# Router logits with the weights held stationary, attention loads issued inside the expert rounds, and key-value products interleaved with their transposes

## The chip, the cores and the metric

One core of one Trainium2 chip. The metric is the device time of one execution in microseconds (us), as the median of several runs. All data are float32; where a product must be exact the kernel splits operands itself.

## What is computed

A two-layer encoder over 16 learned meta tokens followed by 512 frames, width 1024 (48 pad positions in front are inert). Layer 0 is multi-scale retention plus a mixture of experts; after it one shared key/value is projected from the residual stream; layer 1 is sliding-window attention over that shared key/value plus a second mixture of experts; a last RMSNorm follows. The parts that the change touches:

```python
def hier_moe(h, w_group, w_router, w_gate, w_up, w_down):      # twice
    t = h.reshape(-1, d)
    g_probs = jax.nn.softmax(t @ w_group, axis=-1)             # 4 groups
    e_logits = (t @ w_router).reshape(-1, 4, 4)                # 16 experts
    ...                                                        # top group, top 2 experts in it
def shared_kv(x, kv_norm, kv_w, kv_b, pos):                    # once, between the layers
    kv = rms_norm(x, kv_norm) @ kv_w + kv_b                    # 1024 x 512
    ...
q = rope((rms_norm(h, swa_norm) @ w_q + b_q), pos)             # 1024 x 1024
```

## The kernel before

**Tiles and stages.** Tokens lie in five tiles: tile 4, called META, with the 16 meta tokens, and tiles 0 to 3 with 128 frames each. The program runs in this order, each engine with its own hand-written list: retention (four heads, in `head` on every engine); `experts(0)`; the norm before attention, keys and values, queries; attention over four tiles; `experts(1)`; the last norm. Every matrix product needs its input feature-major, so after each norm TensorE transposes a tile in eight blocks into two PSUM banks (`transposed`, L725 to L734), and VectorE multiplies them by the norm's gains into `xT` (`gained`, L1300 and `feature_major`, L1306).

**Banks.** PSUM has 8 banks of 128 x 512. The class `Fills` counts how often each bank was filled and read; `fl.phase` gives names to banks in the order of use, and `wait_full`, `wait_free`, `wait_read` wait on the counts. `norm_plan` (L367) deals the tiles of a norm over four bank pairs.

**The router** (`experts(l)` on TensorE, L868 to L879). All tiles are transposed (L732), then for every tile eight products give its logits, 20 columns (4 groups and 16 experts). The token features `xT` are the stationary operand there and the router weights `wr` the moving one, so that the result is token-major, as VectorE's selection of experts wants it (L1457 on). The selection ends in a rank for every token, an indirect DMA that scatters the rows, and a one-hot product (L890) that builds the rows of round 0 directly. Both kernels have that one-hot product.

**Expert rounds.** 16 rounds of about equal length. In each, two experts with up to 64 rows each are worked on: gate and up product (L913), hidden (L1645), down product (L932). The SyncE queue (SP) loads weights into five slots (`gu`, L449: three lie in `ring`, two in the arena), ahead of the rounds; ScalarE's queue loads rows (L1199) and stores results (L1216). `PASSES` (L42) says which experts a round takes: round k has the second block of expert k-1 and the first of k+1.

**Between the layers.** POOL gathers the experts' results (L1869); per tile VectorE adds them to `h` (L1670, L1672), ScalarE squares (L1069), POOL makes the deviation (L1826, L1829), VectorE scales (L1297), TensorE transposes (L732), VectorE multiplies the transposed tile with the key-value gains into `xTk` and then with the query gains into `xT` (`kv_features`, L1681). When all five tiles are there, TensorE makes keys and values (L959) and then the first tile's queries (L968). SP loads `w_kv` into `ring[:, 0]`, five tables, and the two halves of `w_q` into `ring[:, 1]` and `ring[:, 2]` after the last gathered tile has been used (L697 to L705).

Of the kernel before, what the change touches and what calls it, by code (L numbers as in the profile page):

```python
# [24 lines left out]
META = NT  # L25
# [24 lines left out]
def pass_of(kind, j):  # L50

    return next(p for p, halves in enumerate(PASSES) if (kind, j) in halves)

# [141 lines left out]
def build(nc, a, out):  # L195
# [4 lines left out]
    with ctx:  # L200
# [106 lines left out]
        yo = cv(2, D)  # L307
        th, hid1, hid = cv(2, FF), cv(FF), cv(2, FF)
# [58 lines left out]
        def norm_plan(tag, tiles):  # L367
            fl.phase([(f"{tag}{t}", 2 * (n % 4)) for n, t in enumerate(tiles)])
# [28 lines left out]
        norm_plan("n1_", TILES5)  # L397
        t_norm1 = list(fl.total)
        fl.phase([(f"KV{t}", n) for n, t in enumerate(TILES5)])
        fl.phase([("Qa0", 6), ("Qb0", 7)])  # L400
        fl.phase([(f"KT{t}", (5, 0, 1, 2, 3)[n]) for n, t in enumerate(TILES5)])
# [27 lines left out]
        def sigs(names, tag):  # L429
# [10 lines left out]
            "swa_tables_in", "k_rotated", "V_ready", "VX_zeroed", "VX_ready"))  # L440
        q_rot, m_ready, p_exp, snk_exp, p_scaled, first_parts_used, k_padded, bo_added = (sem(n) for n in (
# [156 lines left out]
        def _(sp):  # L598
# [55 lines left out]
            def experts(l):  # L654
# [43 lines left out]
            sp.dma_start(ring[:, 0], a["w_kv"][0]).then_inc(kv_in, 16)  # L698
            for dst, src in ((stab, a["t_swa"]), (sink_b, a["swa_sinks"][0].partition_broadcast(128)),
                             (kvb, a["kv_b"].partition_broadcast(128)),  # L700
                             (qb, a["swa_b_q"][0].partition_broadcast(128)),
                             (bo, a["swa_b_o"][0].partition_broadcast(128))):
                sp.dma_start(dst, src).then_inc(s_swat, 16)
            for c in range(2):
                sp.dma_start(ring[:, 1 + c], a["w_q"][c]).then_inc(q_in[c], 16)  # L705
# [16 lines left out]
        def _(pe):  # L722
# [145 lines left out]
            def experts(l):  # L868
# [3 lines left out]
                for n, t in enumerate(tiles):  # L872
                    fl.wait_read(pe, f"m{l}_{t}")
                    if n == 0:
                        fl.wait_free(pe, f"LG{l}")
# [1073 lines left out]
```

## Time and profile before

| | |
|---|---|
| median of 3 runs | 1374.65 us (1372.19 to 1377.16) |
| the profiled execution, its own time | 1370.72 us |
| its span, first to last instruction | 1368.7 us |
| mean granted TensorE clock | 0.917 of full |
| TensorE busy (matmul) | 1166.4 us, 85% |
| VectorE, ScalarE, GpSimd busy | 474.0, 244.9, 239.1 us |
| chain that ended last, by engine | PE 66%, issue 12%, DVE 12%, POOL 5%, DMA 3% |
| that chain, lines of this change | L959 3%, L877 2%, L968 4% (with all query products) |

The span counts from the first to the last instruction; what lies around it is 2 us. The chain of waits is followed back from the last instruction, so its shares say what the time consists of; busy shares only say what an engine did meanwhile. "issue" is time in which the engine waited for nothing that the profile shows. In the trace each float32 product of the program is two MATMUL instructions, so that 40 products stand as x80.

### The profile page before, as it was taken

Reading aid. Unit: us, or ns where it says so; the run is one execution under the profiler, and the core shown is the slowest. Engines: PE = TensorE matmul, PEld = TensorE weight load, DVE = VectorE, ACT = ScalarE, POOL = GpSimd, SP = SyncE. Lnnn points to the kernel's source line nnn. Section 1 sums busy time; section 2 is a strip of 40 time slices with the busy share of each in tenths; the row PEclk is TensorE's granted clock in tenths of the full one; section 3 lists DMA queues with packets and bytes.
Section 4 is the critical chain, followed back from the end, with each engine's and each line's share of the span. In section 5 each row is a group of like instructions: output and inputs, shape, how many; then the busy total and the mean of one; then the engine's idle time right before and its main releaser. Section 6 shows DMA issues by size and latency. Waiting matters only on the chain.

```text
span 1368.7 us, 15208 instructions
## 1 busy us (share of the span) xinstructions
PE 1166.4 (85%) x5784; PEld 725.9 (53%) x5784; DVE 474.0 (35%) x847; ACT 244.9 (18%) x453; POOL 239.1 (17%) x168
## 2 busy tenths in 40 slices
PE   4899999999998998489999927877887748999990
PEld 4889889789696776433333313343443343333330
DVE  5301432332258203512222246264554462222224
ACT  4122132132142112000111110021321400101111
POOL 4233233143044221020000044000000002000004
PEclk8999999999999999589999957979999869999995
DMA  6131141041140124649999346300011084999935
GB/s 250 62 139 62 47 154 62 31 169 62 46 154 1 62 82 201 256 142 306 354 346 339 89 154 238 123 0 1 1 67 56 1 338 157 320 355 359 321 86 215
DMA packets 38673, 212.30 MB, mean 155 GB/s; under 512 B 5376, under 2 KB 5504, under 8 KB 29648
## 3 DMA queue, kind: packets, MB, share of 16 engines
q1 hardware_dynamic: 21168, 151.26, 29.8%
q10 hardware_dynamic: 12704, 43.13, 10.2%
q0 software_dynamic: 4736, 17.04, 3.4%
q8 instruction: 41, 0.67, 0.2%
q14 instruction: 24, 0.20, 0.0%
HBM read 307.75 MB, written 35.78 MB: 251 GB/s over the span
## 4 chain that ended last, share of the span: by engine, by line
PE 66%; issue 12%; DVE 12%; POOL 5%; DMA 3%; ACT 2%; ACTq 0%; POOLq 0%; DVEq 0%
PE ps L744 20%; PE ps L913 16%; PE ps L932 8%; PE ps L968 4%; PE ps L1054 4%; POOL ring_r L1838 4%; PE ps L959 3%; PE ps L901 2%; PE ps L877 2%; PE ps L830 2%; DVE xT L1303 1%; DVE arena L1765 1%; DVE arena L1768 1%; PE ps L890 1%; DMA xT<-slot_rows 1%
## 5 line engine op out<-in xcount | busy, mean ns | idle before, releaser
L913 PE MATMUL ps<-ring,xT 128*64 128x512 f32 x640 | 226.9, 598 | 5.9 <-DVE xT L1303 5.9
L744 PE MATMUL ps<-x_hi,ring_r 128*128 128x264 f32 x1024 | 191.3, 287 | 7.0 <-DVE xT_r L1291 7.0
L1838 POOL TENSOR_TENSOR ring_r<-ring,ring_r 128x1024 fp32r<-128x1024 f32 x56 | 134.1, 2408 | 301.9 <-ACT ring_r L1081 301.9
L913 PE MATMUL ps<-arena,xT 128*64 128x512 f32 x384 | 168.7, 592 | 0.0
L744 PE MATMUL ps<-ring_r,x_hi 128*128 128x512 f32 (+1 forms) x480 | 156.2, 407 | 11.6 <-POOL ring_r L1838 11.6
L744 PEld LDWEIGHTS ps<-x_hi,ring_r 128*128 128x128 f32 x1024 | 160.6, 190 | 7.5 <-DVE xT_r L1291 7.3
L1303 DVE TENSOR_TENSOR xT<-ps,gains 128x512 f32<-128x512 f32 (+1 forms) x100 | 62.0, 665 | 249.6 <-PE ps L901 247.3
L744 PE MATMUL ps<-xT_r,ring_r 128*128 128x264 f32 x512 | 146.3, 286 | 0.0
L932 PE MATMUL ps<-arena 128*64 128x512 f32 x512 | 118.6, 606 | 6.1 <-ACT arena L1204 6.1
L913 PEld LDWEIGHTS ps<-ring,xT 128*64 128x64 f32 x640 | 72.9, 138 | 95.4 <-issue 92.0
L744 PEld LDWEIGHTS ps<-ring_r,x_hi 128*128 128x128 f32 (+1 forms) x480 | 84.6, 177 | 43.2 <-POOL ring_r L1838 13.1
L744 PEld LDWEIGHTS ps<-xT_r,ring_r 128*128 128x128 f32 x512 | 97.1, 190 | 0.1
L1869 POOL DMA_INDIRECT arena<-slot_out,slot_i x18 | 17.6, 977 | 413.1 <-DMA slot_out<-arena 408.3
L913 PEld LDWEIGHTS ps<-arena,xT 128*64 128x64 f32 x384 | 52.6, 137 | 54.8 <-issue 54.8
L1081 ACT ACTIVATE ring_r<-ring 128x1024 fp32r<-128x1024 f32 x56 | 57.7, 1052 | 123.7 <-PE ps L744 73.7
L932 PEld LDWEIGHTS ps<-arena 128*64 128x64 f32 x512 | 35.2, 138 | 66.9 <-issue 66.9
L968 PE MATMUL ps<-ring,xT 128*128 128x512 f32 x128 | 60.9, 638 | 9.2 <-DVE arena L1765 9.2
L744 PE MATMUL ps<-ring_r,xT_r 128*128 128x512 f32 (+1 forms) x160 | 65.0, 406 | 0.0
L732 PE MATMUL ps<-con,arena 128*128 128x128 f32 (+1 forms) x152 | 24.5, 324 | 42.0 <-DVE arena L1297 40.2
L1204 ACT ACTIVATE arena<-ps 128x256 f32<-128x256 f32 x32 | 12.3, 384 | 259.2 <-PE ps L920 252.8
L1826 POOL TENSOR_SCALAR var<-ss 128x1 f32<-128x1 f32 (+1 forms) x23 | 9.1, 397 | 262.4 <-ACT arena L1069 254.7
L968 PEld LDWEIGHTS ps<-ring,xT 128*128 128x128 f32 x128 | 25.8, 204 | 42.8 <-issue 42.8
(225 smaller groups left out, 1481.9 us busy)
## 6 DMA issues: line engine op xcount, KB each, us to landing
ring<-in_w_gu SPq DMA_DIRECT2D x46, 2048.0 KB
arena<-in_w_down SPq DMA_DIRECT2D x74, 1024.0 KB
arena<-in_w_gu SPq DMA_DIRECT2D x28, 2048.0 KB
ring<-in_w_ret SPq DMA_DIRECT2D x48, 512.0 KB, 3.6
slot_out<-arena ACTq DMA_DIRECT2D x64, 256.0 KB, 7.1
xT<-slot_rows ACTq DMA_DIRECT2D x60, 256.0 KB, 5.1
slot_rows<-arena ACTq DMA_DIRECT2D x8, 1024.0 KB, 4.1
ring<-in_w_ret_out SPq DMA_DIRECT2D x16, 512.0 KB, 4.5
```

Of the source, the lines that this page charges most:

```text
L744: last = mm(dst, a_parts[x], b_parts[y], start=(start and n == 0), stop=(stop and n == 2))
L830: last = mm(ps[:, b + g, c - lo:HALF], v_tm[0:r, t, 128 * m:128 * m + 128], scores_of(t)[0:r, c - 128 * t:hi - 128 * t], start=(t == 0), s ...
L877: last = mm(ps[0:rows(t), 0, 20 * t:20 * t + 20], xT[:, k, col0(t):col0(t) + rows(t)], wr[:, l, k, :], start=(k == 0), stop=(k == KT - 1))
L901: last = nc.tensor.transpose(ps[:, c // 4, 128 * (c % 4):128 * (c % 4) + 128], xg[:, k % 2, 128 * c:128 * c + 128], ident)
L913: last = mm(ps[cols, b, :], xgT[:, k % 2, c, cols], by_row(gu(j))[:, c, :], start=(c == 0), stop=(c == KT - 1))
L932: last = mm(ps[cols, b, :], hidT[:, c, cols], down[:, j % W_SLOTS, c, 512 * n:512 * n + 512], start=(c == 0), stop=(c == 1))
L959: last = mm(ps[0:rows(t), b, :], xTk[:, k, col0(t):col0(t) + rows(t)], w_kv[:, k, :], start=(k == 0), stop=(k == KT - 1))
L968: last = mm(ps[:, b, :], xT[:, k, col0(t):col0(t) + 128], w_q[c][:, k, :], start=(k == 0), stop=(k == KT - 1))
L1054: last = mm(ps[:, 4 + c, :], oT1[:, k, :], w[:, k, :], start=(k == 0), stop=(k == KT - 1))
L1081: nc.scalar.activation(w_hi[to][:, m], w_raw[slot][:, m], ACT.Copy).then_inc(hi_made, 1)
L1303: return V_.tensor_tensor(dst[:, 4 * g:4 * g + 4, c0:c0 + r], src, gains[:, gain, 4 * g:4 * g + 4].unsqueeze(2).to_broadcast([128, 4, r]), ...
L1838: G.tensor_tensor(w_lo[slot][:, m], w_raw[slot][:, m], w_hi[to][:, m], ALU.subtract).then_inc(lo_made, 1)
```

## The change

It has three parts.

**Router, both layers.** The weights `wr` (20 columns) become the stationary operand and the features the moving one, 128 columns; the logits come out feature-major, 20 x 128, in banks 4 and 5 by turns. ScalarE copies each to `logit_f`, and TensorE transposes them back, one small product per tile, into bank 6. The transposes use two bank pairs instead of four, and the logits of a tile are issued behind the transposes of the next one.

**Loads.** SP issues the five tables in round 8 of layer 0, behind a wait for the scatter; `w_q`'s second half in round 12, `w_kv` in round 13, and `w_q`'s first half in round 15 (`last_use(1)`, `last_use(2)`, `last_use(0)`).

**Keys and values.** The product of a tile is issued behind the transposes of the next one, as in the router. The query features move from VectorE to ScalarE, eight activations of 128 x 128 per tile, with the gain as scale.

```diff
+def last_use(slot):
+    return max(pass_of("second", j) for j in range(slot, EXPERTS, W_SLOTS))
...
+        logit_f = arena[:, cv.at:cv.at + POS]
...
-            norm_plan(f"m{l}_", MOE_TILES[l])
-            fl.phase([(f"LG{l}", 0), (f"RK{l}", 2), (f"X0_{l}", 0)])
+            fl.phase([(f"m{l}_{t}", 2 * (n % 2)) for n, t in enumerate(MOE_TILES[l])])
+            fl.phase([(f"LT{l}_{t}", 4 + n % 2) for n, t in enumerate(MOE_TILES[l])])
+            fl.phase([(f"LG{l}", 6), (f"RK{l}", 2), (f"X0_{l}", 0)])
...
-        norm_plan("n1_", TILES5)
+        norm_plan("n1_", TILES5, 2)
...
@@ SP @@
                 for k in range(ROUNDS):
                     round_full(sp, l, gu_bank(k), k)
                     next_weights(gate_up_weights, k)
+                    beside(k)
...
-            experts(0)
-            sp.wait_ge(mo[0]["gath_used"], 5)
-            (the same loads)
+            def attention_loads(k):
+                if k == EXPERTS // 2:
+                    sp.wait_ge(mo[0]["scattered"], 16 * 2 * 5)
+                    for dst, src in ((stab, a["t_swa"]), (sink_b, ...), (kvb, ...), (qb, ...), (bo, ...)):
+                        sp.dma_start(dst, src).then_inc(s_swat, 16)
+                if k == last_use(2):
+                    sp.dma_start(ring[:, 0], a["w_kv"][0]).then_inc(kv_in, 16)
+                for c in range(2):
+                    if k == last_use(c):
+                        sp.dma_start(ring[:, 1 + c], a["w_q"][c]).then_inc(q_in[c], 16)
+            experts(0, attention_loads)
...
@@ TensorE, experts(l) @@
-                transposed(f"m{l}_", tiles, xn, nrm[f"_m{l}"])
-                for n, t in enumerate(tiles):
-                    fl.wait_read(pe, f"m{l}_{t}")
-                    for k in range(KT):
-                        last = mm(ps[0:rows(t), 0, 20 * t:20 * t + 20], xT[:, k, col0(t):col0(t) + rows(t)],
-                                  wr[:, l, k, :], start=(k == 0), stop=(k == KT - 1))
-                last.then_inc(full[0], 1)
+                def logits(t):
+                    c, b, r = col0(t), fl.bank(f"LT{l}_{t}"), rows(t)
+                    fl.wait_read(pe, f"m{l}_{t}")
+                    fl.wait_free(pe, f"LT{l}_{t}")
+                    for k in range(KT):
+                        last = mm(ps[0:20, b, 0:r], wr[:, l, k, :], xT[:, k, c:c + r], start=(k == 0), stop=(k == KT - 1))
+                    last.then_inc(full[b], 1)
+                def logits_to_tokens(t):
+                    fl.wait_read(pe, f"LT{l}_{t}")
+                    return nc.tensor.transpose(ps[0:rows(t), 6, 20 * t:20 * t + 20], logit_f[0:20, col0(t):col0(t) + rows(t)],
+                                               ident[0:20, 0:20])
+                for n in range(len(tiles) + 1):
+                    if n < len(tiles):
+                        transposed(f"m{l}_", tiles, xn, nrm[f"_m{l}"], tiles[n])
+                    if n:
+                        logits(tiles[n - 1])
+                for t in tiles:
+                    last = logits_to_tokens(t)
+                last.then_inc(full[6], 1)
...
@@ TensorE, keys and values @@
-            transposed("n1_", TILES5, xn1, nrm["_s"])
-            pe.wait_ge(kv_in, 16)
-            all_read(pe, t_norm1)
-            for t in TILES5: (the eight products of a tile)
+            for n in range(len(TILES5) + 1):
+                if n < len(TILES5):
+                    transposed("n1_", TILES5, xn1, nrm["_s"], TILES5[n])
+                if n:
+                    key_values(n - 1, TILES5[n - 1])    # waits kv_in and kv_x_ready >= n
...
@@ ScalarE @@
+            def query_features(n, t):
+                b, c = fl.bank(f"n1_{t}"), slice(col0(t), col0(t) + rows(t))
+                act.wait_ge(kv_x_ready, n + 1)
+                for k in range(KT):
+                    last = nc.scalar.activation(xT[:, k, c], ps[:, b + k // 4, 128 * (k % 4):128 * (k % 4) + 128], ACT.Copy,
+                                                scale=gains[:, G_SWA, k:k + 1])
+                last.then_inc(free[b], 1)
...
@@ VectorE, kv_features @@
-                if t != META:
-                    for gx in range(2):
-                        last = gained(xT, b, gx, G_SWA, col0(t), rows(t))
-                last.then_inc(free[b], 1)
+                last.then_inc(kv_x_ready, 1)
```

How the instructions move on TensorE in the router of layer 0. `con,arena` is a transpose (identity and normed rows), `wr,xT` the old logits; the line numbers of the changed kernel are its own. Before:

```order
1536 L732 MATMUL ps<-con,arena 128x128 x32
1537 L732 MATMUL ps<-con,arena 128x16 x8
1538 L877 MATMUL ps<-wr,xT 128x20 x32
1539 L877 MATMUL ps<-wr,xT 16x20 x8
1540 L883 MATMUL ps<-arena,con 128x80
```

and now:

```order
1536 L748 MATMUL ps<-con,arena 128x128 x16
1537 L892 MATMUL ps<-xT,wr 20x128 x8
1538 L748 MATMUL ps<-con,arena 128x128 x8
1539 L892 MATMUL ps<-xT,wr 20x128 x8
1540 L748 MATMUL ps<-con,arena 128x128 x8
1541 L892 MATMUL ps<-xT,wr 20x128 x8
1542 L748 MATMUL ps<-con,arena 128x16 x8
1543 L892 MATMUL ps<-xT,wr 20x128 x8
1544 L892 MATMUL ps<-xT,wr 20x16 x8
1545 L898 MATMUL ps<-con,arena 128x20 x4
1546 L898 MATMUL ps<-con,arena 16x20
```

The logits' products now start behind two tiles' transposes, and five small transposes (L898) stand at the end.

TensorE between the layers, keys and values (`ring,arena`) and the first queries (`ring,xT`). Before:

```order
1787 L732 MATMUL ps<-con,arena 128x16 x8
1788 L732 MATMUL ps<-con,arena 128x128 x32
1789 L959 MATMUL ps<-ring,arena 16x512 x8
1790 L959 MATMUL ps<-ring,arena 128x512 x32
1791 L968 MATMUL ps<-ring,xT 128x512 x16
```

and now:

```order
1794 L748 MATMUL ps<-con,arena 128x16 x8
1795 L748 MATMUL ps<-con,arena 128x128 x8
1796 L988 MATMUL ps<-ring,arena 16x512 x8
1797 L748 MATMUL ps<-con,arena 128x128 x8
1798 L988 MATMUL ps<-ring,arena 128x512 x8
1799 L748 MATMUL ps<-con,arena 128x128 x8
1800 L988 MATMUL ps<-ring,arena 128x512 x8
1801 L748 MATMUL ps<-con,arena 128x128 x8
1802 L988 MATMUL ps<-ring,arena 128x512 x16
1803 L1005 MATMUL ps<-ring,xT 128x512 x16
```

META's product now stands behind tile 0's transposes, where three tiles' transposes stood before it.

The SP queue in round 8 of layer 0, behind that round's gate and up weights (L643), as it is now (`TENSOR_LOAD e_of` reads an expert's number); before, these five table loads stood behind the last round, at L703:

```order
296 L643 DMA ring<-in_w_gu 128x4096
297 L711 DMA arena<-in_t_swa 128x992 [waits scattered_0]
298 L711 DMA arena<-in_swa_sinks 128x16
299 L711 DMA arena<-in_kv_b 128x512
300 L711 DMA arena<-in_swa_b_q 128x1024
301 L711 DMA arena<-in_swa_b_o 128x1024
302 L664 TENSOR_LOAD e_of [waits bank_full7]
```

They stand now ahead of the next down weights, whose expert number is read from the last row on.

## Rows read from the trace of the kernel before

**Rows 1.** Busy time in two stretches; columns are named in the first row
```profile
core 0: us, PE busy (x) PEld busy (x) DVE busy (x) ACT busy (x) POOL busy (x), PEclk, DMA share, GB/s
545.40:560.00 14.60, 14.46 (x80) 14.32 (x80) 0.04 (x1) 0.00 (x0) 0.00 (x0) 0.50 1.02 429
...
793.00:832.50 39.50, 8.76 (x40) 7.20 (x40) 26.17 (x34) 5.75 (x10) 16.57 (x20) 0.52 0.56 193
```

**Rows 2.** Timeline of PE, router of layer 0: start, duration, instruction, [idle before]
```profile
537.68 3.65 PE L732 MATMUL ps<-con,arena 128*128 128x128 f32 x32
541.61 0.64 PE L732 MATMUL ps<-con,arena 16*128 16x16 f32 x8 [0.27 <-DVE arena L1297]
545.46 14.46 PE L877 MATMUL ps<-wr,xT 128*128 128x20 f32 x80 [3.21 <-DVE xT L1303]
```

**Rows 3.** Timeline of DVE, same place
```profile
538.75 1.29 DVE L1303 TENSOR_TENSOR xT<-ps,gains 128x512 f32<-128x512 f32 x2 [0.17 <-PE ps L732]
```

**Rows 4.** Timeline of PE, router of layer 1
```profile
1097.61 2.81 PE L732 MATMUL ps<-con,arena 128*128 128x128 f32 x24 [1.71 <-issue]
...
1101.71 10.49 PE L877 MATMUL ps<-wr,xT 128*128 128x20 f32 x64
```

**Rows 5.** Prices: the chain of waits (head 0), and one line's instructions (ScalarE)
```profile
280.31 1.78 PE ps L798 x8
...
L1204 ACT ACTIVATE arena<-ps x32: 384/384/386, 615.3 to 1331.7; 128x256 f32<-128x256 f32 x32
```

**Rows 6.** Busy time by microsecond, routers of layers 0 and 1; columns of rows 1
```profile
544.00:545.00 1.00, 0.00 (x0) 0.00 (x0) 1.00 (x3) 0.00 (x0) 0.00 (x0) 1.00 0.91 385
...
546.00:547.00 1.00, 1.00 (x7) 1.00 (x6) 0.00 (x0) 0.00 (x0) 0.00 (x0) 0.50 0.97 410
...
1104.00:1105.00 1.00, 1.00 (x12) 1.00 (x11) 0.25 (x1) 0.00 (x0) 0.00 (x0) 1.00 0.97 401
...
1106.00:1107.00 1.00, 1.00 (x7) 1.00 (x6) 0.00 (x0) 0.00 (x0) 0.00 (x0) 0.50 1.04 442
```

**Rows 7.** Timeline between the layers, all engines
```profile
815.19 1.94 PE L732 MATMUL ps<-con,arena 128*128 128x128 f32 x8 [2.17 <-DVE arena L1297]
...
818.94 1.28 DVE L1303 TENSOR_TENSOR arena<-ps,gains 128x512 f32<-128x512 f32 x2
...
823.95 0.34 SPq L698 DMA_DIRECT2D ring<-in_w_kv  x1
...
826.90 0.74 DVE L1297 TENSOR_SCALAR arena<-h,rstd 128x1024 f32<-128x1024 f32 x1
...
832.58 36.15 PE L959 MATMUL ps<-ring,arena 128*16 128x512 f32 x80 [2.84 <-DVE xT L1303]
```

**Rows 8.** The chain of waits behind them: the first queries
```profile
868.73 13.73 PE ps L968 x32
```

**Rows 9.** DMA issues between the layers: count, KB each, us to landing
```profile
ring<-in_w_q SPq DMA_DIRECT2D x2, 2048.0 KB, 17.6
...
ring<-in_w_kv SPq DMA_DIRECT2D x1, 2048.0 KB, 8.2
```

**Rows 10.** Busy time by round, layer 0, around `gate_up` 11 and 14; columns of rows 1
```profile
724.70:736.39 11.69, 10.88 (x56) 4.05 (x54) 2.65 (x5) 0.77 (x3) 0.00 (x0) 1.00 1.02 359
...
759.77:771.46 11.69, 11.69 (x60) 4.43 (x58) 2.73 (x6) 1.25 (x4) 0.00 (x0) 1.00 0.22 56
```

**Rows 11.** The row loads of layer 0's rounds, and the waits of PE there
```profile
DMA to landing us min/median/max: 3.5/5.7/12.1
...
PE ps L901 <- DMA xT<-slot_rows: 0.8, 1, 0.8
```

**Rows 12.** Timeline at 841 us: POOL's bias additions beside VectorE
```profile
841.17 0.68 DVE L1725 TENSOR_TENSOR arena<-ps,arena 16x512 f32<-16x512 f32 x1 [8.74 <-PE ps L959]
...
842.54 4.88 POOL L1878 TENSOR_TENSOR h<-h,arena 128x1024 f32<-128x1024 f32 x2
842.78 4.78 DVE L1710 TENSOR_TENSOR arena<-arena 16x128 f32<-16x128 f32 x2
```

More of the change, by code:

```diff
@@ L365, in build, with norm_plan @@
         A, B, C, E = 0, 2, 4, 6
-        def norm_plan(tag, tiles):
-            fl.phase([(f"{tag}{t}", 2 * (n % 4)) for n, t in enumerate(tiles)])
+        def norm_plan(tag, tiles, pairs=4):
+            fl.phase([(f"{tag}{t}", 2 * (n % pairs)) for n, t in enumerate(tiles)])
         norm_plan("n0_", TILES5)
@@ L396, in build @@
         moe_plan(0)
-        norm_plan("n1_", TILES5)
[L398 to L401, printed above, removed]
+        norm_plan("n1_", TILES5, 2)
+        fl.phase([(f"KV{t}", 4 + n % 4) for n, t in enumerate(TILES5)])
+        fl.phase([("Qa0", 0), ("Qb0", 1)])
+        fl.phase([(f"KT{t}", (2, 3, 5, 6, 7)[n]) for n, t in enumerate(TILES5)])
         t_kv = list(fl.total)
@@ L652, in first_weights, with experts @@
                         down_weights(l, j, j)
-            def experts(l):
+            def experts(l, beside=lambda k: None):
                 def number(row, j, most):
@@ L694, in _ @@
             first_weights(0, (lambda: out_chunk_used(sp, 2), lambda: None, lambda: out_chunk_used(sp, 3)))
-            experts(0)
-            sp.wait_ge(mo[0]["gath_used"], 5)
[L698 to L705, printed above, removed]
+            def attention_loads(k):
+                if k == EXPERTS // 2:
+                    sp.wait_ge(mo[0]["scattered"], 16 * 2 * 5)
+                    for dst, src in ((stab, a["t_swa"]), (sink_b, a["swa_sinks"][0].partition_broadcast(128)),
+                                     (kvb, a["kv_b"].partition_broadcast(128)),
+                                     (qb, a["swa_b_q"][0].partition_broadcast(128)),
+                                     (bo, a["swa_b_o"][0].partition_broadcast(128))):
+                        sp.dma_start(dst, src).then_inc(s_swat, 16)
[5 more added lines that the diff above has]
+            experts(0, attention_loads)
             fl.wait_full(sp, f"KV{TILES5[-1]}")
@@ L723, in _, with transposed @@
             mm = nc.tensor.matmul
-            def transposed(tag, tiles, src, sig):
+            def transposed(tag, tiles, src, sig, only=None):
                 for n, t in enumerate(tiles):
+                    if only is not None and t != only:
+                        continue
                     r, b = rows(t), fl.bank(f"{tag}{t}")
@@ L1062, in _, with squares @@
         def _(act):
-            def squares(tiles, sig, junk, ready):
+            def squares(tiles, sig, junk, ready, only=None):
                 for n, t in enumerate(tiles):
+                    if only is not None and t != only:
+                        continue
                     ready(t)
@@ L1179, in experts @@
                 squares(MOE_TILES[l], nrm[f"_m{l}"], moe_junk[l], ready)
+                for t in MOE_TILES[l]:
+                    b = fl.bank(f"LT{l}_{t}")
+                    fl.wait_full(act, f"LT{l}_{t}")
+                    nc.scalar.activation(logit_f[0:20, col0(t):col0(t) + rows(t)], ps[0:20, b, 0:rows(t)], ACT.Copy)\
+                        .then_inc(free[b], 1)
                 act.wait_ge(m["eg_in"], 1)
```

23 lines of the change are left out of this document (17 added, 6 removed).

## The prediction

> **What bounds the kernel now.** I read the clock and span first (0.917 granted), then the chain of waits, then the timeline of TensorE at the three places where the diff touches it, then busy time in short stretches there, and last the DMA views. The chain is TensorE for two thirds; in the expert rounds TensorE has no gap, so only stages between them can give something. Three of those are touched. In the router of layer 0, 80 logit instructions take 14.46 us [rows 2], all at half the clock and with TensorE nominally busy [rows 1, 6]: each moves 20 columns and loads 128, so it is paid by the load, 0.18 us apiece. In layer 1 the same 64 take 10.49 us [rows 4], 0.164 apiece; the clock falls halfway through them [rows 6]. Between the layers TensorE does 8.76 us of work in 39.5 [rows 1] and then 36.15 us of key-value products in one piece [rows 7]. Those start at 832.58, right behind VectorE's last features, and `w_kv`, issued at 823.95, needs 8.2 us to land [rows 7, 9]: 832.15. Two waits of nearly equal length end there, so removing only one would give almost nothing; the change removes both.
>
> **Prices.** A 128-block transpose costs 3.65/32 = 0.114 us at full clock [rows 2] and 1.94/8 = 0.243 at half [rows 7]. The new logits move 128 columns over 20 loaded ones. The trace of before has no such form. The nearest row is a float32 product that moves 264 columns, 8 instructions in 1.78 us [rows 5], 0.84 ns a column, so 128 columns are 0.108 us at full clock and twice that, 0.216, at half. I take 0.108, since the row is of the same type, bound by moving as this one will be. From above the bound is 0.164 [rows 4], if the load still counted in full; from below 0.054, half the row. The Trainium skill ("TensorE: Matmul & The Clock Gate", Back-to-back issue gap) gives N/2.4 + 2.5 ns, which is 56 ns for 128 columns; its examples are bf16 and this trace does not agree for float32 (264 columns by it are 113 ns, the row has 222). By its figure the eight full tiles' logits of both layers would be worth 16 x 8 x 0.052 = 6.7 us more.
>
> **Router, layer 0.** A tile is 16 instructions: 16 x 0.108 = 1.73 us. TensorE comes free at 537.68 as before [rows 2]; two tiles' transposes, then it waits for tile 0's features, which VectorE ends at 540.04 [rows 3]. From there: four tiles of logits 6.9; transposes of tiles 2 and 3, 16 x 0.114 = 1.8; META's transposes 0.64 [rows 2]; META's logits, 16 instructions of 16 columns, between 0.2 by columns and 1.8 by the price of a transpose, I take 1.0; ScalarE's copy of the last logits at most 0.38 [rows 5], and five small transposes at 0.114, 0.57. Sum 11.3, so the selection starts at 551.3 where the products ended at 559.92. **-8.6 us.** VectorE's features (1.29 a tile [rows 3]) hide under the 2.6 us that TensorE has per tile; if that cover went, the stage would be 1.3 us a tile, still shorter. ScalarE's other copies hide likewise.
>
> **Router, layer 1.** Tile 0's transposes run 1097.61 to 1098.5; its features are ready at about 1099.8. Then four tiles of logits 6.9, two tiles of transposes 1.8, copy and four small transposes 0.84: 1109.4. Before, 1101.71 + 10.49 = 1112.2 [rows 4]. **-2.8 us**: here the old logits ran half warm and began early.
>
> **Keys and values.** META's product needs META's features, tile 0's transposes on TensorE (end 815.19 + 1.94 = 817.13 [rows 7]) and `w_kv`, now issued in round 13. So the block starts at 817.1 instead of 832.58. It takes the same 36.15 us, which already has a cold beginning (80 x 0.429 = 34.3 by the price of the query products, 13.73/32 [rows 8]; the surplus is four instructions at half clock). Into it go the transposes of tiles 1 to 3, 24 x 0.114 = 2.7 us. End 856.0 instead of 868.73. **-12.7 us.** VectorE must keep ahead: tile 0's key features end by 820.2 and are wanted near 826; tile 3's scaled rows came at 827.64 [rows 7] although VectorE then also made the query features (two pairs of 1.28 before it), and are wanted near 841. ScalarE's eight activations per tile cost at most 8 x 0.38 = 3.1 us [rows 5] against 7.8 us per tile on TensorE, and the first query product waits only for the last tile's, near 847, well before 856. So that move is worth nothing by itself and costs nothing. POOL's bias additions, which waited for the tables, now start near 826 beside VectorE's features. Before, two small VectorE instructions with both inputs in SBUF took 4.78 us beside them, while one that read PSUM kept its 0.68 [rows 12]; the features read PSUM, and even 4.8 us would fit into the slack, so I take nothing. What follows (rotation, transposes of keys) keeps its order and moves as a whole. The moves of `w_q` are worth nothing either: issued at 827 it landed 17.6 us later [rows 9], by 845.
>
> **Loads.** 1.8 MB of tables go into round 8, 2 MB each into rounds 12, 13 and 15. Around `gate_up` 11 the DMA share is 1.02 at 359 GB/s; around 14 it is 0.22 [rows 10]. So the tables and the first weights meet full engines: 1.8 MB at 359 GB/s delay what stands behind them on SP by 5.2 us. The expert weights are issued three rounds, some 35 us, ahead and should bear that. Row loads on ScalarE's queue land in 5.7 us, at worst 12.1, and one of them already made TensorE wait 0.8 us [rows 11]; two or three more rounds are now full. I take +0.6 us, between 0 and 11 (all 4 MB in full rounds coming out as waiting). The new wait for the scatter stands in round 8 and was met in round 1; behind it on SP are only weights with three rounds to spare.
>
> **Sum.** -8.6 - 2.8 - 12.7 + 0.6 = -23.5 us. The profiled execution took 1370.72 us; that gives 1347.2. It lies 3.9 below the median of the runs shown, so the median should be 1351.
>
> **Rivals.** (a) *The clock falls in the routers.* The small products may not hold the clock through the waits. With all logits and later transposes at half clock, layer 0 takes 22.5 us from 540 (13.8 + 3.9 + 1.3 + 2 + 1.5), 2.6 more than before, and layer 1 19.2 from 1099.8, 6.8 more: total -12.7 + 9.4 + 0.6 = -2.7, time 1372. For it: the clock fell in layer 1 some 4 us into the old logits, with TensorE busy all along, and in layer 0 behind 3.2 us of waiting [rows 2, 6]. Against: those instructions moved 20 columns each, the new ones move 128, back to back, and the longest wait left is 0.5 us. A fall halfway gives -13, 1361. (b) *The row loads starve.* For it: full engines and the 12.1 us landing. At its bound of +11 instead of +0.6 the time is 1361. The Trainium skill ("DMA: Bandwidth & Descriptors", Issuing engines are not separate DMA queues) speaks for this one: SP's early loads run on the same engines as ScalarE's row loads and interleave with them, so moving them up takes from the rounds; the share of 1.02 agrees. Against: the delay is once, and the rounds from 14 on are empty. (c) *Slower: cold pieces between the layers.* Cut into pieces with transposes between, the key-value work might never get the full clock. At 0.857 us each, 80 instructions are 68.6 us; with 24 transposes at 0.243 they end at 891.5, 22.8 us later than before; with (a), the whole is +32.8, time 1407. By itself it decides where 23.5/0.43 = 55 of the 80 instructions run at half clock (four did). Against: once started, 7 us stretches of 512-column products follow each other with less than 1 us between. (d) *Nothing changes between the layers*, because `w_kv` or the features come late after all: -10.8, 1364.
>
> **Chances.** Forecast 0.75, partial fall of (a) 0.10, full (a) 0.04, (b) 0.05, (c) 0.03, (d) 0.03. A measurement of this kernel tells some 0.3%, 4.1 us, from no change. Faster is all but full (a) and (c), 0.93; same is full (a), 0.04; slower (c), 0.03. The range goes down to 1344 (logits below my price, less cold at the start of the keys, spread of runs) and up to 1362, where the partial fall and (b) lie.
>
> **What would show it.** Logit instructions near 0.108 us apart with the clock at 1.00 through both routers; selection near 551 and, from the new start of its stage, 2.8 us earlier in layer 1; key-value products from 817 to 856 with the first queries right behind; DMA share above 0.9 until about 760, and no wait of TensorE for weights in the rounds. The forecast is wrong if the clock row of a router reads 0.50 from the first logits on, if TensorE waits for features or for the copy of query features between tiles, or if row-load waits add up to more than 2 us.

## The result and the profile after

The changed kernel takes **1353.05 us**, the median of four runs (1350.47 to 1357.54), where the kernel before took 1373.6 in four. The ratio is 0.9851, with a 95% interval of 0.9823 to 0.988: 20.5 us faster, clearly more than the 0.3% that a measurement of this kernel can tell. A second series of the same kernel gave 1351.16 and 0.985 (0.9827 to 0.9873).

| | before | after |
|---|---|---|
| median of runs, us | 1373.6 | 1353.05 |
| profiled execution: time / span, us | 1370.72 / 1368.7 | 1352.11 / 1350.3 |
| granted TensorE clock | 0.917 | 0.934 |

**Router, layer 0.** The timeline of TensorE in the profile after; it answers to [rows 2], whose logits were one piece of 14.46 us behind a wait of 3.21.

```profile
537.02 1.91 PE L748 MATMUL ps<-con,arena 128*128 128x128 f32 x16
539.43 1.93 PE L892 MATMUL ps<-xT,wr 128*20 128x128 f32 x16 [0.51 <-DVE xT L1364]
541.29 1.09 PE L748 MATMUL ps<-con,arena 128*128 128x128 f32 x8
542.31 1.92 PE L892 MATMUL ps<-xT,wr 128*20 128x128 f32 x16
544.17 1.09 PE L748 MATMUL ps<-con,arena 128*128 128x128 f32 x8
545.19 1.92 PE L892 MATMUL ps<-xT,wr 128*20 128x128 f32 x16
547.04 0.67 PE L748 MATMUL ps<-con,arena 16*128 16x16 f32 x8
547.64 2.31 PE L892 MATMUL ps<-xT,wr 128*20 128x128 f32 x32
549.89 0.51 PE L898 MATMUL ps<-con,arena 20*128 20x20 f32 x5
```

A tile's 16 logit instructions start 1.86 us before what follows them (539.43 to 541.29), 0.116 us each over the tile. Within a tile the single records stand 0.109 us apart; the rest is the change to the next transposes, whose first instruction starts 0.20 us after the last logit. The stage ends at 550.40, 13.38 us after its first transposes start at 537.02; before it was 22.24 (537.68 to 559.92). The busy times by microsecond show why it could: the clock is 1.00 in the middle of the logits, where [rows 6] had 0.50.

```profile
546.00:547.00 1.00, 1.00 (x11) 0.77 (x8) 0.59 (x1) 0.00 (x0) 0.00 (x0) 1.00 0.97 410
548.00:549.00 1.00, 1.00 (x12) 0.92 (x10) 0.10 (x1) 0.00 (x0) 0.00 (x0) 1.00 1.03 434
```

**Router, layer 1.** The same timeline, in pieces that answer to [rows 4]: 12.46 us from 1079.72 to 1092.18, where it was 14.6 (1097.61 to 1112.2).

```profile
1079.72 1.94 PE L748 MATMUL ps<-con,arena 128*128 128x128 f32 x16 [1.68 <-issue]
1082.17 1.92 PE L892 MATMUL ps<-xT,wr 128*20 128x128 f32 x16 [0.51 <-DVE xT L1364]
...
1087.92 3.67 PE L892 MATMUL ps<-xT,wr 128*20 128x128 f32 x32
1091.52 0.66 PE L898 MATMUL ps<-con,arena 20*128 20x20 f32 x4
```

The old logits of this layer ran at both clocks, which gives their price at each. Two stretches of the profile before, with the columns of [rows 1]:

```profile
1102.00:1105.00 3.00, 3.00 (x30) 3.00 (x29) 2.25 (x4) 0.00 (x0) 0.00 (x0) 1.00 0.98 412
1106.00:1112.00 6.00, 6.00 (x30) 6.00 (x29) 0.00 (x0) 0.00 (x0) 0.00 (x0) 0.50 1.05 444
```

Each stretch holds the same number of instructions, those at its edges counted, but the one at full clock lasts 3 us and the one at half 6: by the single records 0.112 and 0.213 us from one to the next. So at full clock the old instruction cost about what the new one costs (0.109). What the changed router saves is the fall of the clock, and hardly anything per instruction.

**Rounds of layer 0.** Here time was lost. The waits of TensorE and the landing of the row loads answer to [rows 11], the chain of waits shows three row loads where the one of before had one (721.17, 12.05 us), and the issues give the landing of the tables and of `w_kv`, which was 8.2 us in [rows 9].

```profile
PE ps L931 <- DMA xT<-slot_rows: 6.2, 5, 2.5
```

```profile
DMA to landing us min/median/max: 3.3/6.9/15.3
```

```profile
687.24 12.21 DMA xT<-slot_rows
...
723.76 12.31 DMA xT<-slot_rows
...
748.68 15.27 DMA xT<-slot_rows
```

```profile
ring<-in_w_kv SPq DMA_DIRECT2D x1, 2048.0 KB, 18.3
...
arena<-in_swa_b_o SPq DMA_DIRECT2D x1, 512.0 KB, 19.4
```

The loads that the change put into rounds 8 and 12 share the engines with expert weights: the DMA share in stretches of 20 us is 1.00 or more from 640 to 760, and what stood there as 0.49 in the last stretch of before (750 to 770) is 1.03 now. Five waits for row loads add up to 6.2 us, where one of 0.8 stood.

```profile
740.00:760.00 20.00, 17.50 (x86) 6.27 (x84) 3.42 (x6) 1.25 (x3) 0.00 (x0) 1.00 1.03 334
760.00:780.00 20.00, 17.77 (x86) 6.31 (x82) 3.57 (x7) 2.58 (x6) 0.00 (x0) 1.00 0.50 166
```

```profile
750.00:770.00 20.00, 20.00 (x104) 7.76 (x102) 3.63 (x7) 1.92 (x5) 0.00 (x0) 1.00 0.49 146
```

(The first fence is the profile after, the second the one before, its 750 to 770.)

**Between the layers.** The timeline after, TensorE, and two instructions of POOL and ScalarE beside it; it answers to [rows 7, 8].

```profile
808.35 1.00 PE L748 MATMUL ps<-con,arena 16*128 16x16 f32 x8 [19.52 <-DVE arena L1358]
```

```profile
820.84 1.09 PE L748 MATMUL ps<-con,arena 128*128 128x128 f32 x8
821.12 9.73 POOL L1936 TENSOR_TENSOR h<-h,arena 128x1024 f32<-128x1024 f32 x4
...
821.77 7.03 PE L988 MATMUL ps<-ring,arena 128*128 128x512 f32 x16
821.97 1.29 DVE L1364 TENSOR_TENSOR arena<-ps,gains 128x512 f32<-128x512 f32 x2 [2.25 <-PE ps L748]
...
823.30 2.18 ACT L1291 ACTIVATE xT<-ps,gains 128x128 f32<-128x128 f32 x8 [3.06 <-DVE arena L1364]
```

```profile
813.46 7.45 PE ps L988 x16
820.91 1.02 PE ps L748 x8
821.93 6.87 PE ps L988 x16
...
837.42 13.74 PE ps L988 x32
851.16 13.73 PE ps L1005 x32
```

The last fence is the chain. The products start at 813.39, 5.04 us behind META's transposes (808.35), where it was 20.56 (812.02 to 832.58), and the queries start 42.8 us behind them instead of 56.7: 13.9 us gained. From the first product to the queries TensorE waits for nothing but its own work: from 813 to 851 it is busy 38.00 of 38.00 us.

Where the 18.4 us of the two spans lie, from marks of the two timelines: start to the end of retention -0.7, router of layer 0 -8.9, from there to the first rows -0.7 (the first products after the one-hot wait run cold for less), rounds of layer 0 +6.5 (198.6 to 205.1, from the first transposes of rows to the end of the last down product), scaled rows 0, keys and values -13.9, attention -0.3, router of layer 1 -2.1, the rest of layer 1 +1.6 (two waits for row loads, 1.7 us, in a part that the change doesn't touch).

### The profile page after: what moved, and what is told of

Read it like the earlier page. It is cut to its first block, busy times and chain, and to the rows that moved or that the text cites. A ratio compares the mean times of both kernels' runs of the same rounds, so it can differ in the third digit from the quotient of the medians.

```text
span 1350.3 us, 15268 instructions
## 1 busy us (share of the span) xinstructions
PE 1152.6 (85%) x5793; PEld 710.4 (53%) x5793; DVE 465.2 (34%) x839; ACT 256.0 (19%) x494; POOL 240.1 (18%) x168
## 4 chain that ended last, share of the span: by engine, by line
PE 64%; issue 12%; DVE 10%; DMA 5%; POOL 5%; ACT 2%; ACTq 1%; POOLq 0%; DVEq 0%
PE ps L760 21%; PE ps L943 14%; PE ps L962 8%; PE ps L1005 5%; PE ps L1091 4%; POOL ring_r L1896 4%; DMA xT<-slot_rows 4%; PE ps L988 3%; PE ps L931 2%; PE ps L846 2%; PE ps L892 1%; DVE arena L1823 1%; DVE arena L1826 1%; PE ps L748 1%; DVE xT L1364 1%
## 5 line engine op out<-in xcount | busy, mean ns | idle before, releaser
L1364 DVE TENSOR_TENSOR xT<-ps,gains 128x512 f32<-128x512 f32 (+1 forms) x92 | 57.4, 665 | 262.3 <-PE ps L931 254.0
L760 PEld LDWEIGHTS ps<-ring_r,x_hi 128*128 128x128 f32 (+1 forms) x480 | 84.5, 177 | 43.1 <-POOL ring_r L1896 13.1
```

Of the source, the lines that this page charges most:

```text
L760: last = mm(dst, a_parts[x], b_parts[y], start=(start and n == 0), stop=(stop and n == 2))
L1364: return V_.tensor_tensor(dst[:, 4 * g:4 * g + 4, c0:c0 + r], src, gains[:, gain, 4 * g:4 * g + 4].unsqueeze(2).to_broadcast([128, 4, r]), ...
```

## The experiments

The theory: the routers and the stage between the layers gain what was predicted, and the early loads give back 5 to 7 us of it in the rounds of layer 0. Its rivals are in the expectations. Ratios are against the kernel before on the same chip; the long stage "rounds" is measured as above in each profile. (The expectations of the runs with parts moved or put last name 181 us before and 187.6 after: those go from round 1's first features to the start of the last down product.)

### Parts of the change alone

**The router alone.** The kernel of the change, with everything between the layers as before:

```diff
-            experts(0, attention_loads)
+            experts(0)
+            sp.wait_ge(mo[0]["gath_used"], 5)
+            sp.dma_start(ring[:, 0], a["w_kv"][0]).then_inc(kv_in, 16)
...
-            for n in range(len(TILES5) + 1):
-                if n < len(TILES5):
-                    transposed("n1_", TILES5, xn1, nrm["_s"], TILES5[n])
-                if n:
-                    key_values(n - 1, TILES5[n - 1])
+            transposed("n1_", TILES5, xn1, nrm["_s"])
```

> The kernel before with the router of the change alone: loads behind the rounds, transposes of all tiles ahead of the key-value products, VectorE's query features. Theory (the routers are worth 8.9 + 0.7 in layer 0 and 2.2 in layer 1, and the rounds lose only what the loads cost): 11.7 us less than before, 1362; rounds of layer 0 near 198.5 as before, META's transposes to the first query 56.5 as before. Rival (the earlier phase of the rounds costs row-load waits by itself): rounds 203 or more, 1366 or more.

Measured: 1360.06 us, ratio 0.9911 (0.9882 to 0.994): -12.2 us. Rounds 200.7 us with 3.0 us of row-load waits; META's transposes to the queries 56.9 us. The theory holds, the rival (rounds of 203 or more) doesn't.

**The loads alone**, in the kernel before:

```diff
-            experts(0)
-
-            sp.wait_ge(mo[0]["gath_used"], 5)
-            sp.dma_start(ring[:, 0], a["w_kv"][0]).then_inc(kv_in, 16)
...
+            experts(0, attention_loads)
```

> The kernel before with the attention loads alone moved into rounds 8, 12, 13 and 15; router and key-value stage are the old ones. Theory (w_kv and the last features both ended near 832 before, so weights alone buy nothing, and the loads cost rounds): from META's transposes to the first key-value product 20.6 us as before, rounds of layer 0 some 4 to 6 us longer, time 1377 to 1380, slower than before. Rival (the loads are where the gain between the layers comes from): the products start earlier, 1365 or less. Third: the old phase of the rounds bears the loads, 1374.

Measured: 1378.72 us, ratio **1.0053** (1.0029 to 1.0077): slower by itself. Its profiled execution (1383.67, in the upper half of its runs, 1376.16 to 1388.83) has rounds of 205.6 us and these waits:

```profile
PE ps L913 <- DMA xT<-slot_rows: 6.4, 6, 1.6
```

and its products start no sooner behind META's transposes (818.39) than before:

```profile
835.39 1.94 PE L744 MATMUL ps<-con,arena 128*128 128x128 f32 x8 [2.35 <-DVE arena L1309]
840.17 37.09 PE L971 MATMUL ps<-ring,arena 128*16 128x512 f32 x80 [2.84 <-DVE xT L1315]
```

With the weights long there, VectorE's last features still end at 840, 21.8 us behind. So the prediction's reading of the two waits of equal length holds: taking only one away gives nothing, and costs what the loads do to the rounds.

**The order alone.** The change with its loads back behind the rounds:

```diff
-            experts(0, attention_loads)
+            experts(0)
+            sp.wait_ge(mo[0]["gath_used"], 5)
+            sp.dma_start(ring[:, 0], a["w_kv"][0]).then_inc(kv_in, 16)
...
```

> The change with all five kinds of attention loads back behind the sixteen rounds of layer 0, behind the wait for the last scaled rows, as in the kernel before; router, order of the key-value products and query features stay changed. Theory (the loads in rounds 8 to 15 delay row loads; in the profile of the change that cost 6.8 us of the rounds): the rounds of layer 0, from round 1's first features to the last down product's start, take about 181 us again instead of 187.6, with row-load waits near 1 us; but w_kv is issued near 813.5 and lands near 821.7, so the products run 822 to 860 instead of 813 to 851. Net +9 against the change: 1362. Rival (the 6.8 us are spread between executions or come from the new router's phase, not from the loads): the rounds stay at 187 us, all is 6.8 later, 1368.

Measured: 1358.84 us, ratio 0.9894 (0.9877 to 0.9911), between the theory's 1362 and the change. Rounds 198.3 us with 2.5 us of waits: the rounds come back. The chain shows what ends the wait between the layers now; the queries start at 858.35, where 860 was expected.

```profile
781.97 3.20 DMA slot_out<-arena
...
810.77 8.36 DMA ring<-in_w_kv
```

**The loads without the order.** The change with all transposes ahead of the products:

```diff
                 if n < len(TILES5):
                     transposed("n1_", TILES5, xn1, nrm["_s"], TILES5[n])
-                if n:
-                    key_values(n - 1, TILES5[n - 1])
+            for n in range(1, len(TILES5) + 1):
+                key_values(n - 1, TILES5[n - 1])
```

> The change with the transposes of all five tiles ahead of the first key-value product; early loads and ScalarE's query features stay. Theory (moving w_kv alone is worth nothing, the products must also start at the first tile's features): the products start when the last tile's key features end, near 824 (17.4 us behind tile 0's transposes as before, less four pairs of query features of 1.28 us), in one piece of 36 us, queries from 860 instead of 851: +9, 1362. Rival (the early weights and the shorter VectorE chain are the gain, the order is worth little): the products start within 4 us of 813, time 1353 to 1357.

Measured: 1361.14 us, ratio 0.9911 (0.9896 to 0.9926); products from 824.33, queries from 859.7, as the theory had it. Together with the router alone these make a square on the new router: neither 0.9911, loads 0.9911, order 0.9894, both 0.985. Loads or order alone give 0 and 2.3 us, both together 8.4. The intervals are some 2 to 4 us to either side, so the 2.3 can't be told from nothing, while the 8.4 can. (The corner with neither had VectorE's query features and the old banks, the other three ScalarE's.) With the loads early and ScalarE's query features the queries did come nearer to META's transposes, 53.1 us instead of 56.9, but the rounds took 202.1 us instead of 200.7.

**The router's order.** The change with all transposes of a router ahead of its logits, in both layers:

```diff
                     if n < len(tiles):
                         transposed(f"m{l}_", tiles, xn, nrm[f"_m{l}"], tiles[n])
-                    if n:
-                        logits(tiles[n - 1])
+                for t in tiles:
+                    logits(t)
```

> The change with all transposes of a router ahead of its first logits (stationary router weights, copies and small transposes stay), in both layers. Theory (most of the gain is the cheaper instruction, the order only fills a wait): in layer 0 the logits start when META's transposes end, near 543.5, take 7.4 + 2.3 us at full clock, and the stage is 3 us longer than in the change, in layer 1 it is 1 us longer: 1357. Rival (without the interleaving the waits between transposes let the clock fall, and the stationary form is no cheaper than the old): the clock row reads 0.50 in the logits, the stage of layer 0 is 8 us or more longer, 1362 to 1366.

Measured: 1359.61 us, ratio 0.9911 (0.9881 to 0.9941), between the theory's 1357 and the rival's 1362. By the ratios that is 8 us more than the change, and the intervals of the two don't meet, so the loss belongs to this kernel and not to one execution of it. The routers account for 2.0 us of it; the most stands in the rounds, which took 210.2 us with 8.4 us of row-load waits, and whose first gate and up products took 9.85 us instead of 8.45 (granted clock 0.82 instead of 1.00 from 590 to 600 us). Why the router's order does this to the rounds is not shown. Its routers:

```profile
542.94 1.86 PE L748 MATMUL ps<-con,arena 128*128 128x128 f32 x16 [1.51 <-DVE xT L1364]
544.74 7.56 PE L892 MATMUL ps<-xT,wr 128*20 128x128 f32 x80
552.22 0.52 PE L898 MATMUL ps<-con,arena 20*128 20x20 f32 x5
...
1093.03 7.17 PE L892 MATMUL ps<-xT,wr 128*20 128x128 f32 x64
```

All at a clock of 1.00. From the retention products' end to the selection's first product it is 21.1 us instead of 19.7 in the change and 28.6 before. So of 8.9 us in layer 0 the interleaving is worth 1.4 within the stage and the rest of the router's change 7.4; in layer 1 (1087.71 to 1100.79, 13.1 us) the interleaving is worth 0.6 of 2.1. The rival's fall of the clock in the waits is out, even with waits of 1.5 us. But the theory's "cheaper instruction" is out too: the 64 logits here take 7.17 us, and 64 of the old ones at their full-clock price of 0.112 would take 7.2 (an estimate). Of the 7.4 us the clock is some 6.9 (14.46 less 64 x 0.112 and 0.4 for META, an estimate). In layer 1 the old logits began without a wait, as these do, and the clock fell in their midst; here it stays. So in layer 1 it stays up with the new form even without the interleaving. Whether the old form would hold it with the interleaving was not tried, and what the clock goes by is not shown.

**VectorE's query features again**, in the change:

```diff
-                for k in range(KT):
-                    last = nc.scalar.activation(xT[:, k, c], ...
...
                 last.then_inc(kv_x_ready, 1)
+                if t != META:
+                    for gx in range(2):
+                        last = gained(xT, b, gx, G_SWA, col0(t), rows(t))
```

> The change with VectorE making the query features again, behind the key features of each tile; ScalarE's part goes. Theory (the move is worth nothing, since TensorE needs 7.8 us a tile and VectorE 2 x 1.28 and the scaling): META's transposes to the first query product 42.6 us as in the change, time within 2 us of 1353. Rival (VectorE's chain sets the pace of the first tiles): TensorE waits for key features between tiles, that stage 3 to 5 us longer, 1356 to 1358.

Measured: 1348.38 us, ratio 0.9841 (0.981 to 0.9873), which can't be told from the change (0.9851, 0.985), though it lies 4.7 us below the 1353 of the expectation. The stage takes 44.2 us from META's transposes to the queries instead of 42.6, and nothing of these 1.6 us is seen in the total. The move is worth nothing that a measurement here, good for some 3 us, can tell.

### The loads

**Tables behind the rounds**, the rest of the change as it is:

```diff
-                if k == EXPERTS // 2:
-                    sp.wait_ge(mo[0]["scattered"], 16 * 2 * 5)
-                    for dst, src in ((stab, a["t_swa"]), ...
...
             experts(0, attention_loads)
+            for dst, src in ((stab, a["t_swa"]), ...
```

> The change with the tables (1.8 MB, issued in round 8) moved behind the sixteen rounds; w_q and w_kv stay in rounds 12, 13 and 15. Theory (any early load that meets full engines costs its share: 1.8 of 5.8 MB at 359 GB/s are 5.2 us of traffic): the wait of the row load in round 8 (12.2 us in the chain at 687) goes, rounds of layer 0 are 2 to 5 us shorter, time 1348 to 1351. Rival (only the weight halves at the end of the full stretch matter, or the loss is spread): rounds within 1 us of 187.6, time 1353.

Measured: 1351.13 us, ratio 0.9841 (0.982 to 0.9861). Rounds 201.2 us with five waits of 4.3 us in all, and the wait that was to go is still there (685.52, 11.98 us in the chain). Against 205.1 that would be the theory's gain, but the repeat of the change below has 201.6: no effect of the tables on the rounds is shown. What they do lengthen is the landing of the row loads in the median, 5.8 us without them against 6.9 and 7.0; that doesn't come out as waiting. Whatever they save in the rounds they also give back: issued at 778 they lie beside the last rows written out, and the gap to META's transposes is 21.7 us instead of 19.5.

**All loads in rounds 14 and 15**, where [rows 10] shows the engines nearly empty:

```diff
-                if k == EXPERTS // 2:
+                if k == ROUNDS - 2:
+                    sp.dma_start(ring[:, 0], a["w_kv"][0]).then_inc(kv_in, 16)
                     sp.wait_ge(mo[0]["scattered"], 16 * 2 * 5)
...
-                for c in range(2):
-                    if k == last_use(c):
+                if k == ROUNDS - 1:
+                    for c in range(2):
                         sp.dma_start(ring[:, 1 + c], a["w_q"][c]).then_inc(q_in[c], 16)
```

> The change with w_kv and the tables issued in round 14 and both w_q halves in round 15, where the engines are nearly empty (share 0.22) and at most one row load is left. Theory: the rounds of layer 0 take 181 us as before the change, w_kv lands well before 806, the products run 37.6 us from there, nothing else moves: 6.8 us less than the change, 1346.5. Rival (the rounds' loss is not from the loads): 1353. Second rival (late w_q halves are missed by the queries): TensorE waits for them behind the products, 1350 or more.

Measured: 1350.93 us, ratio 0.9835 (0.9819 to 0.9851), where the theory had 1346.5. Its step on the rounds came (197.9 us, 2.1 us of waits), its "nothing else moves" did not: the gap from the last down product to META's transposes is 22.9 us instead of 19.5. The chain names the transfer, against 3.21 us in the profile after:

```profile
784.28 6.51 DMA slot_out<-arena
```

**The change again, and `w_q` behind the scaled rows.** The last three kernels were measured side by side on one chip. The first is the unedited change. The second takes the last kernel and puts `w_q` where it was before the change:

```diff
             experts(0, attention_loads)
+            sp.wait_ge(mo[0]["gath_used"], 5)
+            for c in range(2):
+                sp.dma_start(ring[:, 1 + c], a["w_q"][c]).then_inc(q_in[c], 16)
```

The third adds VectorE's query features, the edit shown above.

> The change itself, unedited, to be compared with the two next on one chip and to see how far the row-load waits vary from one execution to the next. Theory (the early loads cost the rounds of layer 0 some 5 us in every execution): rounds 201 to 206 us, against 198 to 201 where the loads are late; time 1353. Rival (205 was an outlier): rounds near 199, time 1347.

> The change with w_kv and the tables in round 14 and both w_q halves behind the last scaled rows, as in the kernel before. With w_q in round 15 the last slot_out write took 6.5 us instead of 3.2 and the gap from the last down product to META's transposes 22.9 us instead of 19.5. Theory (w_q's 4 MB beside that write are the cause): write 3.2 us, gap 19.5, rounds of layer 0 near 198, w_q landed by 825 and wanted near 845, so 3.4 us less than with w_q in round 15: 1347.5. Rival (the tables and w_kv cause it, or the gathers are only moved): gap 22 or more, 1351.

> As the run before, with VectorE making the query features. Theory (the move to ScalarE is worth nothing): within 2 us of that run. Rival (the move to ScalarE costs: the run with VectorE's query features had the lowest median, 1348.4): 3 to 4 us less than that run, 1344.

Measured: 1351.16 (0.985, 0.9827 to 0.9873), **1344.43** (0.9796, 0.9772 to 0.9819) and 1344.78 (0.9797, 0.9773 to 0.9822). The second is 6.7 us better than the change beside it, 3.1 better than expected, the intervals don't meet, and no kernel here is shown to be better. The profiles locate only part of it: rounds 4.0 us shorter (201.6 to 197.6) and the gap behind them 0.2, against 0.5 more before the queries; the change's profiled execution (1347.58) was the fastest of its six. In the second's profile:

```profile
712.00 12.99 DMA xT<-slot_rows
...
783.92 3.20 DMA slot_out<-arena
```

```profile
PE ps L930 <- DMA xT<-slot_rows: 1.8, 2, 0.9
```

```profile
ring<-in_w_q SPq DMA_DIRECT2D x2, 2048.0 KB, 10.7
...
ring<-in_w_kv SPq DMA_DIRECT2D x1, 2048.0 KB, 8.8
```

The write takes 3.2 us again, the gap is 19.3, and `w_kv` lands in 8.8 us instead of 18.3, long before the 807 at which it is wanted. VectorE's query features make no difference here either (1344.78).

The profiled executions together, by where the attention loads go:

| loads of the 16 rounds of layer 0 | rounds, us | row-load waits of TensorE, us | median landing of the 30 row loads, us |
|---|---|---|---|
| none (before; router alone; order alone) | 198.6, 200.7, 198.3 | 0.8, 3.0, 2.5 | 5.5, 6.2, 5.9 |
| `w_kv` and tables in 14, `w_q` in 15 or behind (three kernels) | 197.9, 197.6, 198.7 | 2.1, 1.8, 2.9 | 5.6, 5.5, 5.1 |
| 8, 12, 13, 15 (the change twice; loads without order; VectorE's features; loads alone; router's order) | 205.1, 201.6, 202.1, 201.5, 205.6, 210.2 | 6.2, 4.6, 5.0, 4.7, 6.4, 8.4 | 6.9, 7.0, 7.1, 7.1, 7.1, 7.4 |
| 12, 13, 15, tables behind | 201.2 | 4.3 | 5.8 |

(The landings are medians over all thirty row loads; [rows 11] had 5.7 for 28 of them.) The six without loads before round 14 have a mean of 198.6 us and 2.2 us of waits, the six of the third row 204.3 and 5.9. Early loads cost the rounds 5.7 us, of which 3.7 stand as waits for row loads on TensorE (4.6 us without the kernel of 210.2). The two groups don't overlap, in any column; only the longest landings do (12.1 to 14.1 us against 13.8 to 15.3). Still, one profile of a kernel is only within some 4 us of another of the same.

## Why the prediction came out right

The forecast was 1351 us and a gain of 23.5; it was 20.5 by the medians and 18.6 by the profiled executions. In the profiled executions the sum was off by 5 us: 1347.2 was forecast and 1352.11 came. The loads cost 5.9 us more than the +0.6, and all else together gave back 1. The median came within 2 us of its forecast by luck: the profiled execution of before lay 2.9 us under the median of its four runs (3.9 under that of the three the forecast had), that of the changed kernel 0.9. So the points count more than the sum.

- **Router, layer 0: -8.6, measured -8.9**, and 0.7 more behind it, which the prediction didn't have. The new instruction costs what was forecast (0.109 us against 0.108), and each change between transposes and logits some 0.1 us more, 0.116 per instruction over a tile; META's 16 took 0.39 us (2.31 less 1.92) instead of 1.0. What was misread is the old instruction. "Paid by the load, 0.18 us apiece" is its price at half clock, and there it is 0.213 for the full tiles (META's, at 0.033, pull the mean down); at full clock it is 0.112, and layer 1's 0.164 is a mixture of both. The number came out because the old time was measured and the new clock was rightly taken as full; the reason is the clock and not the load. The order of things is the one described, down to the wait of 0.51 for tile 0's features. By the isolated gap of the Trainium skill ("TensorE: Matmul & The Clock Gate", Back-to-back issue gap), 56 ns, an estimate is that the two routers would have given 128 x 0.053 = 6.8 us more than they did; the section itself gives 81 ns for a sustained stream of 128 columns. The trace agrees with neither for float32: it has 109 ns.
- **Router, layer 1: -2.8, measured -2.1**; the changes between transposes and logits, 0.116 for 64 instructions instead of 0.108, are 0.5 of the difference.
- **Keys and values: -12.7, measured -13.9.** The start, 5.1 us behind META's transposes, came at 5.04. The transposes in between cost what was said; the block lost less to its cold beginning than the old one (the first 16 products 7.52 us, the later ones 7.03; before, four whole instructions). The square above bears out that both waits had to go.
- **Moves called worth nothing.** Query features on ScalarE: shown twice, in two pairs of kernels. POOL's bias additions: they run beside VectorE's features, which keep their 1.29 us (821.12 and 821.97 above), against the slowing of instructions in SBUF that [rows 12] showed. `w_q` early: with both halves in round 15, worth less than nothing. They lengthen the last write, and moving them back behind the scaled rows was worth 5.4 us by the ratios (0.9835 to 0.9796, measured on two chips, the intervals just touching), of which the profiles show 3.6 in the gap (22.9 to 19.3); what the half in round 12 costs by itself was not tried.
- **The step that failed: the loads, "+0.6 us, between 0 and 11".** It is the size that was wrong, 6.5 us in the profile and 5.7 over six kernels, and the forecast's own mark (row-load waits over 2 us) was passed. The error is in the weight of the evidence: [rows 11] had a row load that landed in 12.1 us and one wait of 0.8, which says that the loads of rows stood at the edge of their slack already. What is added in the stretch with a share of 1.02 then comes out in part as waiting (5.8 MB are 16 us of traffic at 359 GB/s and cost 5.7); the argument that the expert weights are three rounds ahead was about the wrong queue. That was rival (b)'s mechanism, and by it 1361 was too much only because the bound put all 4 MB at full price. The Trainium skill ("DMA: Bandwidth & Descriptors", Issuing engines are not separate DMA queues) says that DMAs of different engines run on the same 16 and interleave, and the runs agree: with SP's 5.8 MB there, ScalarE's row loads land in a median of 6.9 to 7.4 us instead of 5.1 to 6.2.
- **The rivals (a), (c) and (d)** are out: the clock reads 1.00 in both routers, the key-value products are at full clock after their first instructions, and the stage gained.

What stays open: why single executions of one kernel differ by 4 us in these rounds, and why the kernel with the router's transposes first lost 5 to 9 us more there than the change. It is also open what holds the clock in the routers, beyond that in layer 1 the new form does it without the interleaving. And 2 us of the 5.7 don't stand as row-load waits; in the change 0.6 of them is a longer wait of the last down product for ScalarE.

## What to carry to other kernels

Where two waits end together, remove both or none, and don't pay for it with a transfer in a stretch whose DMA share is already 1 and on whose small loads the engine nearly waits: look at their waits and at the median of their landing times (here 256 KB, 5.7 us), not at those of the large ones that are issued rounds ahead. A load that is wanted later belongs into the first stretch where the share falls, and behind the small write or read on which the next stage waits. Read the price of an instruction at one clock. With 128 columns loaded and 20 moved it was 0.112 us at full clock and 0.213 at half, the other way round 0.109 at full. Here keeping the operand with few columns in the array and moving the one with many paid because the clock stayed up with it.

## What was not expected of the hardware

- TensorE stood as busy for 14.46 of 14.60 us in the old logits, with a granted clock of 0.50 [rows 1], and in the new ones the clock is 1.00 behind a wait of 0.51 us, and with the transposes first even behind one of 1.51. Busy time alone would not have told the two stretches apart. The same old instruction took 0.112 us in layer 1 before the clock fell and 0.213 behind it.
- A 256 KB write of rows took 6.5 us instead of 3.2 beside 4 MB of weights on another engine's queue (the two halves of `w_q`; the tables were issued 10 us earlier); the next stage waits for the small transfer, and so paid for the large ones.
- META's logits, with 16 columns over 20, started 0.025 us apart (0.39 us for 16), far below the 0.109 of 128 columns.
